# Two transformer blocks on one core: a norm's scale applied before the transposes, the second pair of memory heads inside an output chunk, and the last feed-forward's first chunk computed token tile by token tile

## The chip, the cores and the metric

The kernel runs on one core of one Trainium2 chip. The metric is device time in microseconds (us) of one launch. The kernel before took 786.58 us, the median of 3 runs (784.45, 786.58 and 787.6).

## The reference

256 tokens of width 1024 in fp32 go through two blocks. Block 1 mixes three branches (a gated linear recurrence, an mLSTM, a stick-breaking attention), then has a gated feed-forward of hidden width 2816 and a final norm. Block 2 mixes three other branches, then reads a memory of 256 rows through four heads of width 256, and then has a feed-forward of hidden width 4096 with a squared ReLU:

```python
def second_block(x, mem, ...):
    h = rms_norm(x, pre_mix_g)
    z = h @ w_in                                  # za, zb, zc
    ...
    x = x + rms_norm(y @ w_out, post_mix_g)
    h = rms_norm(x, pre_x_g)
    m = rms_norm(mem, mem_g)
    x = x + rms_norm(memory_cross_attention(h, m, w_xq, w_xkv, w_xo), post_x_g)
    h = rms_norm(x, pre_ffn_g)
    f = square(relu(h @ w_ff1)) @ w_ff2
    return x + rms_norm(f, post_ffn_g)

def memory_cross_attention(h, m, w_q, w_kv, w_o):
    q = (h @ w_q) in 4 heads; k, v = split(m @ w_kv) in 4 heads
    p = softmax(q k^T / 16)
    return (p v) @ w_o
```

`rms_norm(x, g)` is x divided by the root of its mean square over the width, times g.

## The kernel before, in words

**Tiles.** The 256 tokens are two tiles of 128 (t = 0, 1) in `x`. A product needs its input turned, with the model width on the partitions: 8 slices `kt` of 128 channels by 256 tokens, kept in `act_hl` as a rounded part ("high", fp32r) and a remainder ("low"). Quarter q of it holds slices 2q and 2q+1.

**Weights.** `plan_weights` cuts all weight matrices into groups of up to 1 MB, in the order in which they are used. Each group goes through four steps: SyncE loads it into one of 3 `raw` buffers; ScalarE copies it into one of 3 `high` buffers (`split_high`, line 702); VectorE, or GpSimd for some groups of the middle stretch, subtracts to get `low` (`split_low`, line 1217); TensorE uses it (`products`, line 1819) and counts up `w_used`. Each product is three matmuls (low by high, high by low, high by high). A `high` buffer is free when the group three before it is used, and a `raw` buffer when the group three before it has its `low`.

**Chunks.** A chunk is a column block of 512 outputs, in two groups of 4 slices each. `products` has modes: "T" puts tokens on the output's partitions and streams 512 weight columns (48 matmuls per chunk), "C" puts channels there and streams 256 tokens (96 matmuls), "S" is "C" with high and low inputs streamed as one operand, "F" is the second product of a feed-forward, which adds up in banks 4 to 7. `fresh=True` makes TensorE wait for `act_hl` quarter by quarter, `at=(kt, f)` runs f before slice kt's products, and `tile0=True` finishes token tile 0 of the last group ahead of tile 1, so that others can begin on it.

**Order.** All queues are written out by hand, one program per engine. ScalarE and VectorE call `ahead_of(key, mode)` (lines 1060 and 1660), which makes the high or low part of the group two places after each group of the chunk that TensorE is on; `ahead_of_half` does it for one half, and `hold=True` leaves out the last one, which is made later. An engine runs its queue strictly in order, so a group's split stands in front of whatever is written behind it.

**Norm 2** (the input of block 2's mix). After block 1's final norm (`final_norm`, line 1299), ScalarE squares x (`norm_stat(2)`), GpSimd makes `rstd`, and VectorE multiplies the identity by it (`norm_diag(2)`, line 1737) once per token tile. TensorE's `norm` (line 1948), which runs inside the product `("kv", 0)` ahead of slice 7 (line 2227), multiplies x by that diagonal matrix, so that turning and scaling are one matmul per slice and tile. `norm_split(2)` on ScalarE (line 773) and VectorE (line 1277) then makes high and low of `act_hl` from banks 4 to 7. On ScalarE four small transfers are issued at the end of `norm_stat(2)`; on VectorE both halves of `ahead_of(("kv", 0), "C")` come before `norm_split(2)`. The products of `zc` follow.

**Memory heads.** `x_scores(i)`, `x_turn(i)` and `x_out(i)` on TensorE (lines 2138 to 2168) work on heads 2i and 2i+1; between them ScalarE and VectorE do the softmax and the copies. Head h gives quarter h of `act_hl`. `x_scores(0)` runs inside `("xq", 1)`; the rest runs between that chunk and `("xo", 0)`, one after the other, lines 2269 to 2273.

**Feed-forward of block 2.** After the chunks `("xo", 0)` and `("xo", 1)`, ScalarE sums squares per tile (`post_in`), GpSimd makes a root, and VectorE computes the new x (`post_last(1)`, line 1634: `gain`, then `add_normed` in two halves, tile after tile). TensorE does 8 matmuls on the identity (`keep_warm(WARM[3])`, line 2276), turns x in halves as they come (`turn_halves(12)`), and runs the chunks `("up2", c)`, c = 0 to 7, and `("down2", c)`, each one behind. Chunks 0 and 1 of "up2" are in mode "C"; `hidden2(c)` makes ReLU, square, high and low from the two banks.

```python
            x_turn(0)
            x_scores(1)
            x_out(0)
            x_turn(1)
            x_out(1)
            for c in range(2):
                products(("xo", c), "T", fresh=c == 0, tile0=c == 1)
            keep_warm(WARM[3])
            turn_halves(12)
```

## Time and profile before

| what | us |
|---|---|
| median of 3 runs | 786.58 |
| lowest, highest | 784.45, 787.6 |
| the profiled execution, its own time | 784.17 |
| its span, first to last instruction | 782.4 |
| TensorE busy in it | 762.0 (97%) |
| TensorE's granted clock, mean | 0.999 of full |

The span is what the trace shows; the profiled execution's own time has 1.8 us more around it. "Busy" is time in which at least one instruction of the engine was under way. A row of the timeline gives the start, the length, the engine, the line, the operation, output and inputs, how many are merged (x32), and in brackets how long the engine had been idle before it and whom it waited for. Ends of matmuls are modelled: a row's length reaches a little past the start of the next one, so the pace of a run of matmuls is read from start to start. An fp32 matmul shows as two instructions, a transpose as one. Lines are often those of helpers (700 is every ScalarE activation, 1811 every matmul, 1909 every transpose, 1227 every low part), so that a row is told by its tiles.

### The profile page before, as it was taken

How to read it: one execution, taken by the hardware profiler on the slowest of the kernel's cores; microseconds unless marked ns; L12 is line 12 of the kernel's file. 1: busy time of each engine (PE TensorE's matmuls, PEld its weight loads, DVE VectorE, ACT ScalarE, POOL GpSimd, SP SyncE). 2: the span in 40 equal slices, each digit the busy share in tenths (PEclk: the TensorE clock that was granted, in tenths of full speed). 3: DMA queues.
4: the chain of work that ended last, by engine and by line, in shares of the span. 5: the costliest groups of instructions: out<-in, count | busy, mean ns of one | idle time of the engine just before them, and what ended most of it. 6: DMA issues, size and time to landing. Idle time of an engine off the chain costs nothing.

```text
span 782.4 us, 10603 instructions
## 1 busy us (share of the span) xinstructions
PE 762.0 (97%) x4411; PEld 665.8 (85%) x4411; DVE 512.9 (66%) x571; ACT 395.9 (51%) x493; POOL 77.9 (10%) x87
## 2 busy tenths in 40 slices
PE   8999999989999999999999999999999999999996
PEld 8978887868988888888899888789888988888885
DVE  5757964586666666666758989775546555666653
ACT  6375376534544445454554386664446434444441
POOL 3000003020000000000233422020003000000001
PEclk9999999999999999999999999999999999999999
DMA  9554554436465654566465435365234564645431
GB/s 308 186 207 146 176 200 168 155 108 214 154 201 179 208 175 162 165 213 215 164 213 163 162 130 188 117 221 185 103 108 139 212 213 166 211 170 187 164 127 54
DMA packets 74032, 135.67 MB, mean 173 GB/s; under 512 B 4458, under 2 KB 28928, under 8 KB 73984
## 3 DMA queue, kind: packets, MB, share of 16 engines
q1 hardware_dynamic: 72176, 130.80, 49.7%
q10 hardware_dynamic: 1808, 4.19, 1.7%
q8 instruction: 35, 0.57, 0.3%
q14 instruction: 13, 0.11, 0.0%
HBM read 133.93 MB, written 1.05 MB: 173 GB/s over the span
## 4 chain that ended last, share of the span: by engine, by line
PE 85%; DVE 6%; ACT 4%; issue 2%; DMA 2%; POOL 1%; ACTq 0%; DVEq 0%; POOLq 0%
PE wide L1811 60%; PE bank L1811 23%; DVE low L1227 2%; DMA raw<-in_w_in_dram 2%; ACT arena L700 2%; ACT high L700 1%; PE bank L1909 1%; POOL arena L623 1%; DVE act_hl L1283 1%; ACT xn L700 0%; DVE arena L1314 0%; DVE arena L1297 0%; DVE arena L1435 0%; DVE low L1267 0%; ACT act_hl L700 0%
## 5 line engine op out<-in xcount | busy, mean ns | idle before, releaser
L1227 DVE TENSOR_TENSOR low<-raw,high 128x2048 fp32r<-128x2048 f32 (+1 forms) x116 | 261.8, 2280 | 119.0 <-ACT high L700 118.2
L1811 PE MATMUL wide<-act_hl,high 128*128 128x256 f32 (+1 forms) x1248 | 308.7, 328 | 0.0
L700 ACT ACTIVATE high<-raw 128x2048 fp32r<-128x2048 f32 (+1 forms) x130 | 233.9, 1821 | 133.6 <-PE wide L1811 107.8
L1811 PE MATMUL wide<-act_hl,low 128*128 128x256 f32 x864 | 244.7, 283 | 3.1 <-DVE act_hl L1283 2.5
L1811 PEld LDWEIGHTS wide<-act_hl,high 128*128 128x128 f32 x1248 | 210.0, 190 | 22.3
L1811 PEld LDWEIGHTS wide<-act_hl,low 128*128 128x128 f32 x864 | 164.5, 190 | 4.4 <-DVE low L1227 1.6
L1811 PE MATMUL wide<-high,act_hl 128*128 128x512 f32 (+1 forms) x528 | 163.6, 387 | 2.9 <-DVE arena L1435 1.6
L1811 PEld LDWEIGHTS wide<-high,act_hl 128*128 128x128 f32 x528 | 98.2, 188 | 24.3 <-issue 3.7
L1811 PE MATMUL wide<-low,act_hl 128*128 128x512 f32 (+1 forms) x264 | 101.2, 383 | 0.0
L1811 PE MATMUL bank<-high,hid_l 128*128 128x512 f32 x216 | 84.8, 392 | 0.2 <-DVE hid_l L1502 0.2
L1811 PE MATMUL bank<-high,hid_h 128*128 128x512 f32 x216 | 84.4, 391 | 0.0
L1811 PE MATMUL bank<-low,hid_h 128*128 128x512 f32 x216 | 84.2, 390 | 0.0
L700 ACT ACTIVATE arena<-wide 128x512 f32<-128x512 f32 x59 | 32.7, 596 | 90.4 <-PE wide L1811 90.4
L1811 PEld LDWEIGHTS wide<-low,act_hl 128*128 128x128 f32 x264 | 49.6, 188 | 9.1
L553 POOL TENSOR_SCALAR var<-sums 128x1 f32<-128x1 f32 x10 | 7.1, 710 | 482.6 <-ACT arena L700 267.9
L1811 PEld LDWEIGHTS bank<-high,hid_l 128*128 128x128 f32 x216 | 40.6, 188 | 9.2 <-DVE hid_l L1502 0.6
L1811 PEld LDWEIGHTS bank<-high,hid_h 128*128 128x128 f32 x216 | 40.6, 188 | 8.9
L1811 PEld LDWEIGHTS bank<-low,hid_h 128*128 128x128 f32 x216 | 40.6, 188 | 8.0
L1811 PE MATMUL bank<-arena 128*128 128x256 f32 (+8 forms) x256 | 39.2, 341 | 3.2 <-POOL arena L623 1.1
L1314 DVE SCALAR_TENSOR_TENSOR arena<-arena,dw 128x256 f32<-128x256 f32 x60 | 40.2, 712 | 0.9
L1811 PEld LDWEIGHTS bank<-arena 128*128 128x128 f32 (+3 forms) x256 | 32.5, 179 | 9.1 <-POOL arena L623 1.6
L1483 DVE TENSOR_TENSOR arena<-wide,arena 128x512 f32<-128x512 f32 x30 | 20.7, 689 | 29.8 <-ACT arena L700 29.6
(195 smaller groups left out, 662.5 us busy)
## 6 DMA issues: line engine op xcount, KB each, us to landing
raw<-in_w_ff_dram SPq DMA_DIRECT2D x32, 1024.0 KB, 5.3
raw<-in_w_in_dram SPq DMA_DIRECT2D x28, 1024.0 KB, 5.4
raw<-in_w_ffn_in_dram SPq DMA_DIRECT2D x44, 512.0 KB, 4.9
raw<-in_w_ffn_out_dram SPq DMA_DIRECT2D x11, 1024.0 KB, 6.7
raw<-in_w_xkv_dram SPq DMA_DIRECT2D x8, 1024.0 KB, 5.1
raw<-in_w_o_dram SPq DMA_DIRECT2D x4, 1024.0 KB, 5.1
raw<-in_w_out_dram SPq DMA_DIRECT2D x4, 1024.0 KB, 5.2
raw<-in_w_xq_dram SPq DMA_DIRECT2D x4, 1024.0 KB, 4.9
```

What stands on the lines that cost most here:

```text
L553: pool.tensor_scalar(v, sums[:, t, 0:1], sums[:, t, 1:2], EPS, ALU.add, ALU.add)\
L623: pool.affine_select(out=part_a, in_=part_a, compare_op=ALU.is_gt, fill=0.0, base=0, pattern=[[0, 4], [1, P]], channel_multiplier=-1).then ...
L700: return act.activation(dst, src, func, **k)
L1227: tt(part(low, g), part(raw, g), f32(part(high, g)), SUB).then_inc(sem.low_by_dve, 1)
L1283: ins = stt(l_, bank[4 + q][:, k * T:(k + 1) * T], col(NORM_GAIN[n], kt), f32(h_), MUL, SUB)
L1314: ins = stt(tile_of(dst, c), window, weight(j, c), tile_of(dst, c), MUL, ADD)
L1483: tt(in2(h_low[b]), wide_of(b, 0), in2(h_low[b]), ADD).then_inc(sem.hid_sum, 1)
L1811: return pe.matmul(dst, lhs, rhs, start=start, stop=stop, skip_group_check=loose)
L1909: return pe.transpose(dst, src, ident[0:n, 0:n])
```

## The change

Three places change.

1. **Norm 2.** VectorE's `norm_diag(2)` gives way to `scale_x()`, which writes x times `rstd` into `xn`, one instruction of 128x1024 per token tile. TensorE turns `xn` with 16 transposes (`turn_scaled`) at the same point, ahead of slice 7 of `("kv", 0)`. ScalarE makes the high part of zc's first group ahead of `norm_stat(2)`, and issues its four small transfers (`load_block2`) behind the high part of the second. VectorE makes only the first low part ahead of `norm_split(2)` and the second behind it.
2. **Heads.** `x_turn(1)` and `x_out(1)` move into `("xo", 0)`, ahead of slices 2 and 4. `x_scores` waits for its own head's queries alone. VectorE and ScalarE put the splits of the next groups between the halves.
3. **Feed-forward.** `keep_warm(WARM[3])` goes. `("up2", 0)` is computed with tokens on the partitions, first all of tile 0 and then all of tile 1 (`up_by_token`); the turns of tile 1's halves stand inside it. Its result is squared by token (`hidden_tok`), turned by 8 transposes inside `("up2", 1)` (`turn_hidden`), and split from there (`hidden_turned`). ScalarE and VectorE split `act_hl` by token tile (`split_tile`), VectorE's first two quarters of tile 0 ahead of `add_normed` of tile 1. The splits of both groups of `("up2", 0)` now come before `post_last(1)`, as `hold` is gone.

```diff
-WARM = 4, 4, 6, 8
+WARM = 4, 4, 6
@@ scalar
+            def split_tile(t):
+                if t == 0:
+                    act.wait_ge(sem.w_used, me.used)
+                tok = slice(t * P, (t + 1) * P)
+                for q in range(4):
+                    act.wait_ge(sem.turned, me.seen("turned"))
+                    for k in range(2):
+                        kt = 2 * q + k
+                        ins = f(split_of(kt, False)[0][:, tok], bank[4 + q][:, k * T + t * P:k * T + (t + 1) * P], ACT.Copy,
+                                scale=col(NORM_GAIN[5], kt))
+                    ins.then_inc(sem.act_h, 1)
...
             norm_stat(FINAL)
+            ahead_of_half(("kv", 0), 0)
             norm_stat(2)
-            ahead_of_half(("kv", 0), 0)
             ahead_of_half(("kv", 0), 1)
+            load_block2()
             norm_split(2)
...
             x_out(0)
+            ahead_of_half(("xo", 0), 0)
             x_turned(1)
             x_out(1)
-            for c in range(2):
-                ahead_of(("xo", c), "T", hold=c == 1)
-                post_in(c)
-            split_high(me.used + LEAD)
-            norm_split(5)
+            ahead_of_half(("xo", 0), 1)
+            post_in(0)
+            ahead_of(("xo", 1), "T")
+            post_in(1)
+            split_tile(0)
+            split_high(me.used + LEAD + 1)
+            split_tile(1)
             norm_stat(5)
+            ahead_of(("up2", 0), "T")
+            hidden_tok()
+            ahead_of_half(("up2", 1), 0)
+            hidden_turned()
+            ahead_of_half(("up2", 1), 1)
+            hidden2(1)
+            ahead_of(("down2", 0), "F")
@@ vector
+            def scale_x():
+                for t in range(TT):
+                    dve.wait_ge(sem.rstd, me.seen("rstd"))
+                    ts(xn[:, t, :], x[:, t, :], rstd[:, 4 + t:5 + t], None, MUL).then_inc(sem.scaled, 1)
...
-            norm_diag(2)
-            ahead_of(("kv", 0), "C")
+            scale_x()
+            ahead_of_half(("kv", 0), 0)
             norm_split(2)
+            ahead_of_half(("kv", 0), 1)
...
-            x_out()
-            ahead_of(("xo", 0), "T")
+            x_out(0)
+            ahead_of_half(("xo", 0), 0)
+            x_out(1)
+            ahead_of_half(("xo", 0), 1)
             post_first()
-            ahead_of(("xo", 1), "T", hold=True)
-            post_last(1)
-            norm_split(5, (0, 1))
-            split_low(me.used + LEAD)
-            norm_split(5, (2, 3))
+            ahead_of(("xo", 1), "T")
+            post_last(1, lambda: split_tile(0, (0, 1)))
+            split_tile(0, (2, 3))
+            split_low(me.used + LEAD + 1)
+            split_tile(1, range(4))
             dve.wait_ge(sem.rstd, me.seen("rstd", TT))
+            ahead_of(("up2", 0), "T")
+            hidden_tok()
+            ahead_of_half(("up2", 1), 0)
+            hidden_turned()
+            ahead_of_half(("up2", 1), 1)
+            hidden2(1)
+            ahead_of(("down2", 0), "F")
@@ tensor
+            def turn_scaled():
+                for t in range(TT):
+                    pe.wait_ge(sem.scaled, 0 + t + 1)
+                    turn_x(t, range(KD), t == 1, xn)
+
+            def up_by_token():
+                pair = 2 * (me.pairs % 2)
+                parts = chunks[("up2", 0)]
+                for t in range(TT):
+                    tok = slice(t * P, (t + 1) * P)
+                    for g, kts in parts:
+                        if t == 0 and kts[0]:
+                            turn_half(1, 0)
+                        pe.wait_ge(low_sem(g), before(g))
...
+                            if kt % 2 == 0:
+                                pe.wait_ge(sem.act_hl, me.seen("act_hl"))
...
+                        if t:
+                            ins.then_inc(sem.w_used, 1)
+                        elif kts[0]:
+                            ins.then_inc(sem.tok_used, 1)
+                            turn_half(1, 1)
...
-                    pe.wait_ge(sem.xq_in, 2 + 2 * (h // 2))
+                    pe.wait_ge(sem.xq_in, h + 1)
...
-            products(("kv", 0), "C", is_mem=True, at=(KD - 1, norm))
+            products(("kv", 0), "C", is_mem=True, at={KD - 1: turn_scaled})
...
             x_out(0)
-            x_turn(1)
-            x_out(1)
+            products(("xo", 0), "T", fresh=True, at={2: lambda: x_turn(1), 4: lambda: x_out(1)})
+            products(("xo", 1), "T", tile0=True)
             for c in range(2):
-                products(("xo", c), "T", fresh=c == 0, tile0=c == 1)
-            keep_warm(WARM[3])
-            turn_halves(12)
+                turn_half(0, c)
+            up_by_token()
+            products(("up2", 1), "C", at={4: turn_hidden})
+            pe.wait_ge(sem.hid_hl, n1 + 2)
+            products(("down2", 0), "F", 0, last=False)
             n2 = F2 // NB
-            for c in range(n2 + 1):
+            for c in range(2, n2 + 1):
```

## Rows read from the trace of the kernel before

**Rows 1.** The page's first part: busy us, share of the span, instructions of each engine.
```profile
PE 762.0 (97%) x4411; PEld 665.8 (85%) x4411; DVE 512.9 (66%) x571; ACT 395.9 (51%) x493; POOL 77.9 (10%) x87
```

**Rows 2.** Timeline of TensorE at norm 2, 392 to 400 us.
```profile
393.23 3.74 PE L1811 MATMUL bank<-diag,x 128*128 128x128 f32 x32
396.73 0.36 PE L1811 MATMUL wide<-hid_h,low 128*128 128x256 f32 x1
...
398.12 0.28 PE L1811 MATMUL wide<-hid_h,high 128*128 128x256 f32 x1
399.83 0.36 PE L1811 MATMUL wide<-act_hl,low 128*128 128x256 f32 x1 [1.44 <-DVE act_hl L1283]
```

**Rows 3.** Timeline of TensorE, 16 transposes inside another product, 520 to 524 us.
```profile
522.04 1.91 PE L1909 MATMUL bank<-ident,x 128*128 128x128 f32 x16
523.70 0.48 PE L1811 MATMUL wide<-high,hid_l 128*128 128x512 f32 x1
```

**Rows 4.** Timelines of VectorE, ScalarE and GpSimd at norm 2, 386 to 402 us.
```profile
393.97 4.94 DVE L1227 TENSOR_TENSOR low<-raw,high 128x2048 fp32r<-128x2048 f32 x2 [1.69 <-ACT high L700]
398.82 3.21 DVE L1283 SCALAR_TENSOR_TENSOR act_hl<-bank,vec,act_hl 128x256 fp32r<-128x256 f32 x8
...
392.02 3.71 ACT L700 ACTIVATE high<-raw 128x2048 fp32r<-128x2048 f32 x2 [1.03 <-issue]
395.73 3.03 ACT L700 ACTIVATE act_hl<-bank,vec 128x256 fp32r<-128x256 f32 x8
...
391.38 0.57 POOL L564 TENSOR_TENSOR rstd<-var,neg_half 128x1 f32<-128x1 f32 x1
```

**Rows 5.** Groups by line and shape, VectorE: a TENSOR_SCALAR from SBUF to SBUF.
```profile
L1386 DVE TENSOR_SCALAR arena<-arena 128x512 f32<-128x512 f32 x1 | 0.4, 421 | 0.0
```

**Rows 6.** Timeline of TensorE at the memory heads, 556 to 571 us.
```profile
557.73 7.17 PE L1811 MATMUL bank<-arena 128*128 128x256 f32 x32 [0.54 <-DVE arena L1297]
564.74 1.04 PE L1909 MATMUL bank<-ident,arena 128*128 128x128 f32 x8
566.57 3.72 PE L1811 MATMUL bank<-arena 128*128 128x256 f32 x16 [0.79 <-ACT arena L700]
569.93 0.58 PE L1811 MATMUL wide<-high,act_hl 128*128 128x512 f32 x1
```

**Rows 7.** Timeline of VectorE at the heads: the low part of quarter 0.
```profile
564.00 0.68 DVE L1447 SCALAR_TENSOR_TENSOR act_hl<-bank,act_hl 128x512 fp32r<-128x512 f32 x1
```

**Rows 8.** Timeline of TensorE between the chunks xo and up2, 588 to 600 us.
```profile
591.94 1.95 PE L1811 MATMUL bank<-ident 128*128 128x128 f32 x16
593.72 2.38 PE L1909 MATMUL bank<-ident,x 128*128 128x128 f32 x16
597.21 0.35 PE L1811 MATMUL wide<-act_hl,low 128*128 128x256 f32 x1 [1.11 <-DVE act_hl L1283]
```

**Rows 9.** Timelines of VectorE, ScalarE and GpSimd in the same stretch.
```profile
591.26 1.41 DVE L1628 SCALAR_TENSOR_TENSOR x<-xn,rstd,x 128x512 f32<-128x512 f32 x2 [0.44 <-POOL rstd L564]
...
597.76 2.28 DVE L1227 TENSOR_TENSOR low<-raw,high 128x2048 fp32r<-128x2048 f32 x1
...
590.20 0.30 POOL L553 TENSOR_SCALAR var<-sums 128x1 f32<-128x1 f32 x1 [59.90 <-ACT arena L700]
...
599.47 0.66 POOL L556 TENSOR_SCALAR var<-sums 128x1 f32<-128x1 f32 x1 [5.60 <-ACT xn L700]
```

**Rows 10.** The chain that ended last: chunks xo 0 and 1 ("T"), up2 0 and 1 ("C").
```profile
570.29 21.81 PE wide L1811 x96
...
597.21 23.27 PE wide L1811 x192
```

**Rows 11.** Timeline of TensorE, 170 to 173 us: a stretch of transposes and waiting.
```profile
170.39 1.09 PE L1909 MATMUL bank<-ident,xn 128*128 128x128 f32 x8
172.61 0.47 PE L1811 MATMUL wide<-high,act_hl 128*128 128x512 f32 x1 [1.13 <-DVE act_hl L1447]
```

**Rows 12.** Busy us of each engine in 166 to 173 us; PEclk is the granted clock.
```profile
166.00:173.00 7.00, 5.87 (x30) 4.63 (x30) 4.94 (x9) 1.86 (x3) 3.18 (x3) 1.00 0.35 129
```

More of the change, by code:

```diff
@@ L147, in __init__ @@
         self.hid_t = new("hid_t")
+        self.hid_turned = new("hid_turned")
         self.ident = new("ident")
@@ L202, in __init__ @@
         self.rstd = new("rstd")
+        self.scaled = new("scaled")
         self.sb_a = new("sb_a")
@@ L213, in __init__ @@
         self.sumsq = new("sumsq")
+        self.tok_used = new("tok_used")
         self.turned = new("turned")
@@ L785, in norm_split, with hidden_tok, hidden_turned @@
                     ins.then_inc(sem.act_h, 1)
+            def split_tile(t):
[9 more added lines that the diff above has]
+                    ins.then_inc(sem.act_h, 1)
+            def hidden_tok():
+                for t, b in enumerate(me.pair()):
+                    if t:
+                        act.wait_ge(sem.w_used, me.used)
+                    else:
+                        act.wait_ge(sem.tok_used, 1)
+                    f((h_act, h_tmp)[t], b[:, :], ACT.Relu).then_inc(sem.hid_t, 1)
+            def hidden_turned():
+                act.wait_ge(sem.hid_a, me.seen("hid_a", 2))
+                for b in range(2):
+                    act.wait_ge(sem.hid_turned, b + 1)
+                    f(flat(hid_h[0][:, 2 * b:2 * b + 2, :]), bank[4 + b][:, :], ACT.Copy).then_inc(sem.hid_h, 1)
             def first_stat(t):
@@ L1288, in norm, with split_tile @@
                 norm_split(n)
+            def scale_x():
+                for t in range(TT):
+                    dve.wait_ge(sem.rstd, me.seen("rstd"))
+                    ts(xn[:, t, :], x[:, t, :], rstd[:, 4 + t:5 + t], None, MUL).then_inc(sem.scaled, 1)
+            def split_tile(t, quarters):
+                tok = slice(t * P, (t + 1) * P)
+                for q in quarters:
+                    dve.wait_ge(sem.act_h, me.seen("act_h"))
+                    for k in range(2):
+                        kt = 2 * q + k
+                        h_, l_ = (half[:, tok] for half in split_of(kt, False))
+                        ins = stt(l_, bank[4 + q][:, k * T + t * P:k * T + (t + 1) * P], col(NORM_GAIN[5], kt), f32(h_), MUL, SUB)
+                    ins.then_inc(sem.act_hl, 1)
             def rep_wait():
@@ L1452, in turn_merged, with x_out @@
                     low_of_bank(q, 0.5)
-            def x_out():
-                for q in range(4):
+            def x_out(i):
+                for q in (2 * i, 2 * i + 1):
                     low_of_bank(q)
@@ L1524, in hidden2, with hidden_tok, hidden_turned @@
                     dve.wait_ge(sem.hid_hl, me.seen("hid_hl"))
+            def hidden_tok():
+                for t in range(TT):
+                    h = (h_act, h_tmp)[t]
+                    dve.wait_ge(sem.hid_t, me.seen("hid_t"))
+                    tt(h, h, h, MUL).then_inc(sem.hid_a, 1)
+            def hidden_turned():
+                for b in range(2):
+                    dve.wait_ge(sem.hid_h, me.seen("hid_h"))
+                    tt(flat(hid_l[0][:, 2 * b:2 * b + 2, :]), bank[4 + b][:, :], f32(flat(hid_h[0][:, 2 * b:2 * b + 2, :])), SUB)\
+                        .then_inc(sem.hid_hl, 1)
+                dve.wait_ge(sem.hid_hl, me.seen("hid_hl", 2))
             def za_in():
@@ L1632, in post_first, with post_last @@
                     gain(b, t, 0)
-            def post_last(i):
+            def post_last(i, then=None):
                 for t, b in enumerate(me.pair()):
                     gain(b, t, 1)
+                    if t and then:
+                        then()
                     add_normed(i, t)
@@ L1956, in norm, with turn_x @@
                             ins.then_inc(sem.turned, 1)
-            def turn_x(t, kts, last):
+            def turn_x(t, kts, last, src=x):
                 for kt in kts:
                     o = (kt % 2) * T + t * P
-                    ins = turn(bank[4 + kt // 2][:, o:o + P], x[:, t, kt * P:(kt + 1) * P])
+                    ins = turn(bank[4 + kt // 2][:, o:o + P], src[:, t, kt * P:(kt + 1) * P])
                     if last and kt % 2:
@@ L2169, in _ @@
             turn_start()
-            products("lru", "C", fresh=True, at=(6, rep_made))
+            products("lru", "C", fresh=True, at={6: rep_made})
             vectors()
@@ L2264, in _ @@
             pe.wait_ge(sem.zg, 2)
-            products(("kv", 3), "T", is_mem=True, at=(4, lambda: turn_all(10)))
-            products(("xq", 0), "C", fresh=True, at=(4, rep_made))
+            products(("kv", 3), "T", is_mem=True, at={4: lambda: turn_all(10)})
+            products(("xq", 0), "C", fresh=True, at={4: rep_made})
             pe.wait_ge(sem.kv_in, 8)
-            products(("xq", 1), "C", at=(4, lambda: x_scores(0)))
+            products(("xq", 1), "C", at={4: lambda: x_scores(0)})
             x_turn(0)
```

49 lines of the change are left out of this document (33 added, 16 removed).

## The prediction

> **What bounds the kernel now.** I read the page's first part first: TensorE is busy 762.0 of 782.4 us, VectorE 66% and ScalarE 51% [rows 1]. So time is to be had from only two sources: work that TensorE does and need not do, and its few waits. I then went through TensorE's timeline for the rows with a bracket (a wait) and read the three places of the change, with the other engines' timelines beside it to see what each wait hangs on.
>
> Norm 2: 32 instructions on the diagonal, 393.23 to 396.73, the last products of ("kv", 0), then a wait on VectorE until 399.83 [rows 2]. VectorE spends 4.94 us on two low parts and only then, at 398.82, splits the quarter for which TensorE waits, though ScalarE has offered it since some 396.5 (start 395.73, two of eight instructions in 3.03) [rows 4]. Heads: a wait of 0.54 for scaled queries and one of 0.79 for ScalarE's copies [rows 6]. Feed-forward: from 591.94 to 597.21 TensorE does matmuls on the identity, 16 transposes that come as x comes, and waits 1.11 [rows 8].
>
> **Part 1, norm 2.** *TensorE's work.* 32 diagonal instructions from start to the next start: 3.50 us [rows 2]. 16 transposes of the same size inside another product: 522.04 to 523.70, 1.66 us [rows 3]. Saved: 1.84.
>
> *Is the scaled x there in time?* GpSimd has the second root at 391.38 + 0.57 = 391.95 [rows 4]. No row shows a TENSOR_SCALAR of 128x1024. A 128x512 one takes 0.42 [rows 5], so twice that, 0.84, is the upper bound if the pace holds, and 0.42 the lower one; I take 0.7. It ends at 392.7, and TensorE asks at 393.23. Covered by the products of slices 0 to 6; the cover is 0.5 us wide. (ScalarE's high part, moved ahead of the squares, takes 3.71/2 = 1.86 us [rows 4] and delays the first root; the second tile's square waits for VectorE's final norm anyway, so I leave the second root where it is.)
>
> *The wait.* The first quarter is turned after 10 of 16 transposes, 393.23 + 1.04 = 394.3. ScalarE ended its squares at 392.02 - 1.03 = 391.0 [rows 4]. Now it makes zc's second high part (to 392.9) and issues the four transfers, which before fitted under a square and that 1.03 of idle; if they run one behind the other they end at 394.7. Its first quarter is then ready at about 395.3 (2 x 0.38). VectorE makes one low part from 392.7, 2.3 us, to 395.0, splits at once (2 x 0.40) and is done at 396.2. TensorE ends ("kv", 0) at 393.23 + 1.66 + (398.24 - 396.73) = 396.4. The wait of 399.83 - 398.24 = 1.59 (the bracket's 1.44 plus modelled ends) goes.
>
> *What is late next.* zc's second low part now comes behind the split, from 398.7 to 401.0; TensorE needs it half a chunk after 396.4, at 402.2. 1.2 us to spare. GpSimd's masks come some 3 us later and nothing waits on them for 30 us. Gain 1.84 + 1.59 = 3.4; I take 3.3, with ends 2.8 (scaling at 1.3 a tile, the transfers in the open) and 3.4.
>
> **Part 2, heads.** With h + 1 in the wait, x_scores(1) starts one scaling instruction sooner: 0.54 gone. x_turn(1) and x_out(1) cost TensorE what they cost now, but the wait of 0.79 for two copies [rows 6] lies under slices 2 and 3 (12 matmuls, 21.81/96 = 0.227 each, 2.7 us [rows 10]). New is that slice 0 needs quarter 0 at once: its low part ends at 564.68 [rows 7], and TensorE is free of x_out(0) at 564.74 [rows 6]; both move alike, so 0 to 0.1 is lost. Quarter 2 is asked for right after x_out(1): its head is done 1.8 us earlier (half of 3.36, 566.57 to 569.93), copy and low part take 0.6 and 0.69, so it is there 0.4 us before. Gain 1.33 less 0.1: 1.2, ends 0.9 and 1.33.
>
> **Part 3, feed-forward.** All in the old frame, with the chunk xo ending at 591.94. Without `hold`, up2's second low part (2.28 us [rows 9]) runs on VectorE as soon as the first half of ("xo", 1) is used, 591.94 - 5.45 = 586.5: high to 588.4, low to 590.7. Behind it in VectorE's queue stands `gain` for tile 0, whose sum was there at 590.20 [rows 9]: 0.55 us late. GpSimd's root waits with it. The row shows why: the same small operation takes 0.30 at 590.20 and 0.66 at 599.47, where it ends as VectorE's low part ends [rows 9]. So tile 0's halves of x come at 592.4 and 593.1 instead of 591.96 and 592.67.
>
> By the Trainium skill (GPSIMD Engine Reference, Specifications) GpSimd shares its SBUF interfaces with VectorE, with contention where VectorE has two SBUF inputs; that speaks against this part of the change. The 0.66 row agrees. Without the rule the root would come 0.4 sooner and the sum would gain 0.4.
>
> TensorE turns the halves up to 593.6 (8 transposes, 0.10 each). ScalarE's first two 128-token copies end about 593.5 (0.25 to 0.38 each), VectorE's gain of tile 1 at 593.75, its two half-size split instructions (0.2 to 0.4 each, half of 0.40 and all of it) at about 594.3. up2 starts at 594.4 instead of 597.21: 2.8 earlier.
>
> Then TensorE's own bill. The eight transposes of tile 1 move inside the chunk, +0.83; the eight of `turn_hidden` are new, +0.83; the chunk in "T" instead of "C" saves (23.27 - 21.81)/2 = 0.73 [rows 10]. Net +0.93. Tile 1 must be in time: VectorE's queue behind 594.3 is a quarter (0.5), add_normed (1.41), two quarters (1.1), a low part (2.3), four quarters (2.2), 7.5 us in all, to 602.4 at the latest pieces; TensorE reaches tile 1's last quarters at 603.5. 1.1 us to spare. `hidden_tok` and the splits of ("up2", 1) end before TensorE gets to slice 4 of that chunk at about 612. Gain 2.8 - 0.9 = 1.9; I take 1.8. Low end 0.6 (the slack used up once), high end 2.2.
>
> Sum: 3.3 + 1.2 + 1.8 = 6.3 us. The profiled execution took 784.17, so 777.9 in its terms. It lies 2.4 below the median of the runs, 786.58; from there the same gain gives 780.3. A measurement of this kernel can tell about 0.5%, 3.9 us, from no change; the threshold is 782.65.
>
> **Rivals.**
> *A, the clock falls (slower).* The plain matmuls on the identity go, and from 591.94 to 594.4 TensorE only waits or transposes, 2.46 us. If the granted clock then fell from 2.4 to 1.2 GHz for the chunk that follows, its 10.9 us would double and the sum turn to 6.3 - 10.9 = -4.6: 791.2. It decides for "slower" from 6.3 us of work at the lower clock on. Against it: from 170.39 to 172.61 there are 8 transposes and a wait and no other matmul, 2.2 us, and the clock stays at 1.00 [rows 11, 12]. The new stretch is 0.24 longer than that, and would be longer still if VectorE is late.
> The Trainium skill speaks for it (TensorE: Matmul & The Clock Gate, PE-mode transpose): transposes do not count as busy for the clock as matmuls do. By that rule the whole of both stretches is idle; the 1.00 in the row shows that 2.2 us of it are borne. I give it 0.06.
>
> *B, part 1 is eaten.* The middle stretch leans on VectorE, which also shares ports with GpSimd's low parts there; if zc's second low part comes later than 402.2, or the later collisions fall worse, the 3.3 shrink to nothing and 3.0 remain: 783.6. Against: VectorE's work there hangs on the end of zc's products and should move with it. 0.12.
>
> *C, part 3 gives nothing.* The queue order (low part before gain, split before add_normed) makes TensorE wait inside the chunk for tile 1: 4.5 remain, 782.1. 0.14.
>
> *D, the change does not do what it says,* transposes of xn costing what the diagonal did (-1.84) and waits merely moving: total 2 or less, 784.6 or more. Rows 3 speak against. 0.06.
>
> **How the numbers follow.** Forecast 0.62. Small ends of the parts: 2.8 + 0.9 + 0.6 = 4.3, 782.3; large ends 3.4 + 1.33 + 2.2 = 6.9, 779.7. The runs scatter by 2.1 below and 1.0 above their median, so a median of a few by about 1.5. The range reaches from 778.2 to 784.2: it takes in B and C and leaves out A and most of D. Faster by over 0.5%: forecast, most of C, a third of B, 0.74. Within: the rest of B, C, D, 0.20. Slower: A, 0.06.
>
> **What would show it.** Right: 16 transposes and no bank<-diag instruction at norm 2, and less than 0.2 us before zc's first matmul; no bracket over 0.2 at the heads, x_out(1) inside ("xo", 0); up2's first matmul 2.3 to 2.7 us behind xo's last; clock 1.00 there. Wrong: a bracket on tile 1's quarters or on a low part inside zc or up2; new waits of TensorE between 450 and 500 us; a total that moves by under 4 us with all three places as described.

## The result, and the profile after

| | before | after |
|---|---|---|
| median, us (runs) | 784.45 (5) | 778.45 (5) |
| lowest, highest | 784.15, 787.6 | 777.98, 780.04 |
| profiled execution | 784.17 | 777.98 |
| its span | 782.4 | 776.2 |

The ratio is 0.9919, 95% interval 0.9902 to 0.9936: faster by 0.8%. In a second set of runs the changed kernel gave 778.06 (777.95 to 780.06, 5 runs) beside 784.62, ratio 0.9919 [0.9907, 0.9932]; one execution of the kernel before in that set took 2681.08 us and is left out of the ratio. Profiled execution against profiled execution the gain is 784.17 - 777.98 = 6.2 us; the forecast was 6.3. The time forecast, 780.3, is 1.85 too high all the same: it was counted down from 786.58, and the kernel before does not stand there (its two further runs gave 784.4 and 784.15).

The page's first part of the changed kernel; against [rows 1] TensorE has 72 instructions and 3.4 us of work less:

```profile
PE 758.6 (98%) x4339; PEld 660.3 (85%) x4339; DVE 514.0 (66%) x579; ACT 396.9 (51%) x501; POOL 74.3 (10%) x87
```

**Norm 2.** Timelines of TensorE, then VectorE, of the changed kernel, to be held against [rows 2 to 5]:

```profile
393.08 1.91 PE L1995 MATMUL bank<-ident,xn 128*128 128x128 f32 x16
394.75 0.36 PE L1897 MATMUL wide<-hid_h,low 128*128 128x256 f32 x1
...
396.33 0.36 PE L1897 MATMUL wide<-act_hl,low 128*128 128x256 f32 x1
```

```profile
391.95 0.76 DVE L1337 TENSOR_SCALAR xn<-x,rstd 128x1024 f32<-128x1024 f32 x1 [0.76 <-POOL rstd L567]
392.62 2.29 DVE L1271 TENSOR_TENSOR low<-raw,high 128x2048 fp32r<-128x2048 f32 x1
395.31 3.23 DVE L1327 SCALAR_TENSOR_TENSOR act_hl<-bank,vec,act_hl 128x256 fp32r<-128x256 f32 x8 [0.40 <-ACT act_hl L703]
398.45 2.28 DVE L1271 TENSOR_TENSOR low<-raw,high 128x2048 fp32r<-128x2048 f32 x1
```

The 32 instructions of 3.50 us are 16 transposes of 1.67, and zc's first matmul has no bracket. VectorE splits at 395.31 where it split at 398.82, since one low part (392.62) and not two stand ahead of it; the other comes at 398.45.

**Heads.** TensorE, against [rows 6]: no bracket, and x_turn(1) stands between matmuls of the output chunk.

```profile
552.71 1.04 PE L1995 MATMUL bank<-ident,arena 128*128 128x128 f32 x8
553.69 7.17 PE L1897 MATMUL bank<-arena 128*128 128x256 f32 x32
560.79 0.47 PE L1897 MATMUL wide<-high,act_hl 128*128 128x512 f32 x1
...
563.63 1.03 PE L1995 MATMUL bank<-ident,arena 128*128 128x128 f32 x8
564.42 0.48 PE L1897 MATMUL wide<-high,act_hl 128*128 128x512 f32 x1
```

**Feed-forward.** TensorE, VectorE and GpSimd, against [rows 8, 9]:

```profile
586.83 0.39 PE L1897 MATMUL wide<-high,act_hl 128*128 128x512 f32 x1
587.85 1.32 PE L1995 MATMUL bank<-ident,x 128*128 128x128 f32 x8 [0.63 <-DVE x L1702]
589.80 0.47 PE L1897 MATMUL wide<-high,act_hl 128*128 128x512 f32 x1 [0.63 <-DVE act_hl L1346]
...
592.61 0.60 PE L1995 MATMUL bank<-ident,x 128*128 128x128 f32 x4
592.97 0.48 PE L1897 MATMUL wide<-high,act_hl 128*128 128x512 f32 x1
```

```profile
583.82 2.29 DVE L1271 TENSOR_TENSOR low<-raw,high 128x2048 fp32r<-128x2048 f32 x1 [2.05 <-ACT high L703]
586.03 0.69 DVE L1694 TENSOR_TENSOR xn<-wide,row_g 128x512 f32<-128x512 f32 x1
587.04 1.42 DVE L1702 SCALAR_TENSOR_TENSOR x<-xn,rstd,x 128x512 f32<-128x512 f32 x2 [0.32 <-POOL rstd L567]
```

```profile
585.32 0.96 POOL L556 TENSOR_SCALAR var<-sums 128x1 f32<-128x1 f32 x1 [58.47 <-ACT arena L703]
```

The warming matmuls are gone, two waits of 0.63 stand in their place, and the chunk up2 begins 2.97 us behind xo's last matmul (before: 5.50). The turns of tile 1 stand inside it, without a wait. GpSimd's small operation begins as ScalarE has its sum and takes 0.96: it ends at 586.28, shortly behind VectorE's low part (583.82 + 2.29 = 586.11). In the kernel before, where no low part runs beside it, it takes 0.30 [rows 9].

**Where the time went.** Each stretch from start to start in the timelines of TensorE: from the first matmul of ("kv", 0) to zc's first, from x_turn(0) to xo's last matmul, from there to up2's first, from there to down2's first.

| stretch | before | after | difference | forecast |
|---|---|---|---|---|
| norm 2 | 16.67 | 13.32 | -3.35 | -3.3 |
| zc to x_turn(0) | 156.32 | 156.38 | +0.06 | 0 |
| heads and xo | 35.56 | 34.12 | -1.44 | -1.2 |
| xo to up2 | 5.50 | 2.97 | -2.53 | -2.8 |
| up2 to down2 | 23.10 | 24.31 | +1.21 | +0.93 |

These add up to 6.05 us. The other 0.15 of the 6.2 lies ahead of norm 2, where nothing was changed: ("kv", 0) begins at 383.01 and not 383.16. Behind down2's first matmul both kernels take 154.96 to the last one.

### The profile page after: what moved, and what is told of

Read it like the earlier page. It is cut to its first block, busy times and chain, and to the rows that moved or that the text cites. A ratio compares the mean times of both kernels' runs of the same rounds, so it can differ in the third digit from the quotient of the medians.

```text
span 776.2 us, 10478 instructions
## 1 busy us (share of the span) xinstructions
PE 758.6 (98%) x4339; PEld 660.3 (85%) x4339; DVE 514.0 (66%) x579; ACT 396.9 (51%) x501; POOL 74.3 (10%) x87
## 3 DMA queue, kind: packets, MB, share of 16 engines
HBM read 133.93 MB, written 1.05 MB: 174 GB/s over the span
## 4 chain that ended last, share of the span: by engine, by line
PE 88%; DVE 5%; ACT 2%; DMA 1%; POOL 1%; issue 1%; DVEq 0%; ACTq 0%; POOLq 0%
PE wide L1897 63%; PE bank L1897 24%; PE bank L1995 2%; DMA raw<-in_w_in_dram 1%; ACT arena L703 1%; DVE low L1271 1%; ACT high L703 1%; POOL arena L626 1%; DVE x L1702 0%; DVE act_hl L1327 0%; DVE arena L1373 0%; DVE arena L1494 0%; DVE low L1311 0%; DVE xn L1694 0%; DVE arena L1624 0%
## 5 line engine op out<-in xcount | busy, mean ns | idle before, releaser
L1897 PE MATMUL wide<-act_hl,high 128*128 128x256 f32 (+1 forms) x1184 | 297.2, 330 | 0.0
L1897 PE MATMUL wide<-act_hl,low 128*128 128x256 f32 x832 | 235.8, 283 | 0.5 <-DVE low L1311 0.5
L1897 PEld LDWEIGHTS wide<-act_hl,high 128*128 128x128 f32 x1184 | 200.1, 190 | 22.3
L1897 PE MATMUL wide<-high,act_hl 128*128 128x512 f32 (+1 forms) x560 | 174.7, 388 | 3.4 <-DVE arena L1494 1.6
L1897 PEld LDWEIGHTS wide<-act_hl,low 128*128 128x128 f32 x832 | 158.5, 190 | 1.6 <-DVE low L1311 0.7
L1897 PEld LDWEIGHTS wide<-high,act_hl 128*128 128x128 f32 x560 | 104.2, 188 | 26.4 <-issue 4.5
L1897 PE MATMUL wide<-low,act_hl 128*128 128x512 f32 (+1 forms) x280 | 107.5, 384 | 0.0
L1897 PEld LDWEIGHTS wide<-low,act_hl 128*128 128x128 f32 x280 | 52.7, 188 | 9.6
```

Of the source, the lines that this page charges most:

```text
L1897: return pe.matmul(dst, lhs, rhs, start=start, stop=stop, skip_group_check=loose)
```

## The experiments

### Each part alone

Both edits of norm 2 were tried one at a time on the kernel before.

```diff
@@ n2_turn: the transposes, without the new order
-            norm_diag(2)
+            scale_x()
...
-            products(("kv", 0), "C", is_mem=True, at=(KD - 1, norm))
+            products(("kv", 0), "C", is_mem=True, at=(KD - 1, turn_scaled))
@@ n2_order: the order, with the diagonal
-            norm_stat(2)
             ahead_of_half(("kv", 0), 0)
+            norm_stat(2)
             ahead_of_half(("kv", 0), 1)
+            load_block2()
...
-            ahead_of(("kv", 0), "C")
+            ahead_of_half(("kv", 0), 0)
             norm_split(2)
+            ahead_of_half(("kv", 0), 1)
```

> The kernel before with the scaled x turned plainly, and all orders of ScalarE and VectorE as before. Theory S (VectorE's queue set the wait): TensorE saves 1.84 us of work ahead of the last products of (kv, 0) but still waits for VectorE, which makes both low parts first; zc starts at 399.8 as before, the bracket grows from 1.44 to about 3.2, and the whole time is unchanged to 0.2 us. Rival W (the work itself was the cost): zc starts 1.8 us sooner, at 398.0.

> The kernel before with only the new order of ScalarE and VectorE at norm 2 (one low part ahead of the split, one behind it, the high part ahead of the squares, the four transfers later); the diagonal matmuls stay. Theory S: the wait of 1.44 (1.6 from start to start) goes, zc starts at 398.3, 1.5 to 1.6 us sooner, and the total falls by as much. Together with the other half that makes 3.4, where the halves alone give 0 and 1.6. Rival W: the order gives nothing by itself, the diagonal's 3.5 us being what made VectorE late; zc at 399.8.

`n2_turn` took 786.84 us (783.96 to 789.16, 10 runs), ratio 1.0018 [1.0002, 1.0034]. TensorE got its 1.8 us back and spent them on the same wait, behind which its clock fell. Timeline of TensorE, then busy time in windows of 2 us (the last three columns are the granted clock, the DMA share and GB/s):

```profile
395.01 0.36 PE L1817 MATMUL wide<-hid_h,low 128*128 128x256 f32 x1
...
399.96 0.56 PE L1817 MATMUL wide<-act_hl,low 128*128 128x256 f32 x1 [3.28 <-DVE act_hl L1284]
```

```profile
398.00:400.00 2.00, 0.04 (x1) 0.07 (x1) 2.00 (x4) 2.00 (x6) 1.43 (x2) 0.82 0.88 317
400.00:402.00 2.00, 2.00 (x9) 2.00 (x10) 2.00 (x6) 1.54 (x1) 0.00 (x0) 0.50 1.02 380
```

zc's first matmul came 16.69 us behind ("kv", 0)'s (before: 16.67), and the clock went from 2.4 to 1.2 GHz until 406 us, so that x_turn(0) stood 159.0 behind it and not 156.3. With the wait of 1.44 [rows 2] the kernel before has 1.00 in all these windows. `n2_order` took 783.48 (782.68 to 784.66, 6 runs), ratio 0.998 [0.9967, 0.9994]: the stretch is 15.08, 1.59 less, with no bracket. Alone the transposes give nothing and the order 1.59; together they give 3.35. That is part 1's sum of 1.84 and 1.59, but only in this pair.

```diff
@@ heads_only: on the kernel before
+            ahead_of_half(("xo", 0), 0)
             x_turned(1)
             x_out(1)
...
-                    pe.wait_ge(sem.xq_in, 2 + 2 * (h // 2))
+                    pe.wait_ge(sem.xq_in, h + 1)
...
-            x_turn(1)
-            x_out(1)
...
+            products(("xo", 0), "T", fresh=True, at=(2, lambda: x_turn(1), 4, lambda: x_out(1)))
@@ ff_only: on the kernel before, all of part 3
-            keep_warm(WARM[3])
-            turn_halves(12)
...
+            up_by_token()
+            products(("up2", 1), "C", at={4: turn_hidden})
```

> The kernel before with only the heads' part of the change. Theory S: two waits go, the span falls by 1.2 to 1.4 us, and the chunk xo ends 1.2 to 1.4 us sooner after the start of xq. Rival: the fp32 matmuls of the head put between fp32r products slow both, and less than 0.8 is left.

> The kernel before with only the feed-forward's part of the change. Theory S as corrected by the trace after: up2 starts 2.5 to 2.7 us sooner after xo's last matmul (2.7 instead of 5.3), 1.2 us of that are spent again up to the start of (down2, 0), and the span falls by 1.3 to 1.5 us. Rival (the parts lean on each other): alone it gives less than 0.8, since the heads' part is what makes VectorE free in time.

`heads_only` took 784.34 (782.32 to 784.99, 10 runs), 0.9985 [0.9974, 0.9995]; `ff_only` 784.15 (782.76 to 785.13, 10 runs), 0.9988 [0.9977, 0.9998]. Their traces have the stretches of the changed kernel: 34.12 for heads and xo in the one, 2.97 and 24.35 for xo to up2 and up2 to down2 in the other. So the two parts don't lean on each other: -1.44, and 27.32 - 28.60 = -1.28. The medians alone (0.40 and 0.59 under 784.74) would have made the parts look like a third and a half of that: six and five of the ten executions have a mean clock of 0.995 or 0.996, and these lie 1 to 2 us above the others.

### The clock between xo and up2

```diff
@@ no_warm: on the kernel before
-            keep_warm(WARM[3])
@@ warm_back: on the changed kernel, ahead of tile 0's turns
             products(("xo", 1), "T", tile0=True)
+            keep_warm(8)
```

> The kernel before without the eight matmuls on the identity behind xo. From xo's last product to up2's first, 5.2 us, TensorE then only turns x and waits. Rival A of the prediction (the clock falls): the granted clock drops to 1.2 GHz behind that stretch, matmuls of 512 columns step by more than 0.4 us instead of 0.23 for a while, and the kernel is slower than before by 1 us or more. Theory S: the clock stays at 1.00, the transposes wait for x as before, and the time changes by less than 0.2 us.

> The changed kernel with the eight matmuls on the identity put back behind xo. Theory S: they take 1.8 us, x's first half is ready after 0.8 of them, so up2 starts 0.9 to 1.1 us later than in the changed kernel and the span grows by that, at the same clock. Rival A: they keep the clock up, and the span is equal or shorter.

`no_warm` took 786.38 (784.53 to 788.05, 10 runs), 1.0014 [1.0, 1.0028]. Timeline of TensorE, then its windows:

```profile
592.61 1.32 PE L1909 MATMUL bank<-ident,x 128*128 128x128 f32 x8
595.32 1.32 PE L1909 MATMUL bank<-ident,x 128*128 128x128 f32 x8 [1.39 <-DVE x L1628]
597.75 0.55 PE L1811 MATMUL wide<-act_hl,low 128*128 128x256 f32 x1 [1.11 <-DVE act_hl L1283]
```

```profile
596.00:598.00 2.00, 0.89 (x5) 0.68 (x6) 1.27 (x4) 2.00 (x6) 0.00 (x0) 0.79 0.10 39
598.00:600.00 2.00, 2.00 (x10) 2.00 (x11) 2.00 (x2) 2.00 (x6) 0.00 (x0) 0.50 0.67 223
600.00:602.00 2.00, 2.00 (x17) 2.00 (x16) 2.00 (x5) 2.00 (x3) 1.73 (x4) 0.86 0.24 33
```

Rival A's mechanism is real: behind 5.1 us of transposes and waits the clock goes to 0.50, and up2 to down2 grows from 23.10 to 24.35. By the Trainium skill (TensorE: Matmul & The Clock Gate, Part 4, PE-mode transpose) transposes do not count as busy for the clock the way matmuls do. The trace agrees with that and does not prove it: the two waits alone, 1.39 and 1.11, are shorter than the one of 2.11 us at 41.98 us, behind which the clock of the same trace stays at 1.00. What the forecast had too large is the price, 1.25 us and not 10.9: the clock is back at 0.86 in the window from 600 us and at 1.00 in the next. In the changed kernel the same stretch is 2.97 long and the clock stays:

```profile
588.00:590.00 2.00, 1.36 (x9) 0.92 (x9) 2.00 (x6) 1.61 (x7) 1.14 (x2) 1.00 0.96 393
590.00:592.00 2.00, 2.00 (x10) 1.64 (x10) 2.00 (x6) 2.00 (x4) 0.00 (x0) 1.00 0.18 72
```

`warm_back` took 779.63 (779.11 to 780.78, 4 runs), 0.9929 [0.9911, 0.9947]: up2's first matmul stands 3.91 behind xo's last, 0.94 later, and the clock is 1.00 as it was without. By token tiles the warmers are all cost.

### What sets up2's first matmul

```diff
@@ quarters_first: on the changed kernel
-            post_in(1)
-            split_tile(0)
+            post_in(1, lambda: split_tile(0, (0, 1)))
+            split_tile(0, (2, 3))
...
-                    gain(b, t, 1)
                     if t and then:
                         then()
+                    gain(b, t, 1)
@@ low_late: on the changed kernel
-            ahead_of(("xo", 1), "T")
+            ahead_of(("xo", 1), "T", hold=True)
             post_last(1, lambda: split_tile(0, (0, 1)))
+            split_low(me.used + LEAD)
```

> The changed kernel with ScalarE's copies of tile 0's quarters 0 and 1 ahead of its squares of tile 1, and VectorE's split of them ahead of tile 1's gain. Theory Q (the queue order of ScalarE and VectorE sets the start of up2): up2 starts at 588.8 instead of 589.8, 1.0 us sooner; tile 1's x then comes 1.1 us later, at 591.2 to 591.9, TensorE waits up to 0.5 for it inside the chunk, and 0.4 to 0.8 us of the span remain. Rival: the wait only moves inside the chunk and the span is the same to 0.2 us.

> The changed kernel with VectorE's low part of up2's second group put behind add_normed of tile 1 instead of ahead of tile 0's gain. Theory Q: gain of tile 0 starts at 585.3 instead of 586.03, GpSimd's first operation takes 0.3 instead of 0.96 us, and x's first half is ready 0.7 us sooner; but the low part ends at 593 to 594.5 and pushes quarters 2 and 3 behind it, so that TensorE waits 1.5 to 2.5 us at slice 4: slower by 1 to 2 us in all. Rival: the low part fits into VectorE's idle time there and the span falls by 0.5.

`quarters_first` took 779.22 (778.65 to 780.57, 4 runs), 0.9924 [0.9906, 0.9942]: up2's first matmul stands 2.98 behind xo's last, as in the changed kernel, so neither tile 1's gain nor ScalarE's order is what it waits for, and behind it 0.39 is lost. `low_late` took 780.26 (779.21 to 781.8, 4 runs), 0.9934 [0.9909, 0.9959]. Its rows of GpSimd, then TensorE's rows with a bracket:

```profile
587.33 0.30 POOL L556 TENSOR_SCALAR var<-sums 128x1 f32<-128x1 f32 x1 [58.49 <-ACT arena L703]
```

```profile
591.33 0.47 PE L1898 MATMUL wide<-high,act_hl 128*128 128x512 f32 x1 [0.82 <-DVE act_hl L1346]
...
595.89 0.47 PE L1898 MATMUL wide<-high,act_hl 128*128 128x512 f32 x1 [1.11 <-DVE act_hl L1346]
```

With VectorE's low part out of the way GpSimd's operation takes 0.30 in place of 0.96 and up2 begins 2.50 behind xo, 0.47 sooner. Two things come sooner here, the root and tile 0's gain (by 0.77, as it stood behind the same low part); the bracket of 0.32 on the root in the changed kernel says that GpSimd was the later of the two there. The low part then stands ahead of tile 0's later quarters: TensorE waits 1.11 inside the chunk, up2 to down2 takes 25.72 and not 24.31, and the kernel ends 0.94 later than the changed one. The 0.96 agrees with the rule on shared SBUF interfaces that the forecast named (the Trainium skill, GPSIMD Engine Reference, Specifications); the forecast's own row for it was 0.66. The 0.30 at 587.33 has a VectorE instruction beside it too, the gain at 587.26, but one that reads a bank and only one input from SBUF.

### Two levels of time

In all sets of runs so far some executions lie 1.5 to 2 us above the rest, about two in three of them at a mean clock of 0.996 or less, where those of the rest are 0.997 to 0.999. A mean of 0.997 by itself says nothing: the trace of `both` below has it without a fall, because the clock is at 0.50 in the last 4 us, where TensorE has no work left, and that of `before_warm_41` has it with one. Two places that the change does not touch showed a fall. One is behind a wait in the first 42 us. Timeline and windows of `quarters_first`, where nothing of this had been edited:

```profile
41.95 0.60 PE L1997 MATMUL bank<-ident,arena 128*4 128x128 f32 x4 [2.05 <-ACT arena L703]
```

```profile
42.00:44.00 2.00, 2.00 (x9) 1.60 (x10) 1.95 (x3) 0.01 (x1) 0.00 (x0) 0.67 0.78 297
44.00:46.00 2.00, 2.00 (x7) 1.52 (x6) 0.00 (x0) 1.95 (x3) 0.00 (x0) 0.50 0.86 238
```

The same wait is 2.11 us in `no_warm`, and there the clock stays at 1.00: it falls in some executions and not in others. The first remedy was matmuls on the identity in that wait, alone on both kernels, and in `best` together with an edit of the section before, VectorE's low part cut in halves around tile 0's quarters.

```diff
@@ warm_41 (on the changed kernel), before_warm_41 (on the kernel before)
             products("ifsv", "T", width=264)
+            keep_warm(7)
             if_rows()
@@ best: the changed kernel, keep_warm(7) as above, and
-            ahead_of(("xo", 1), "T")
+            ahead_of(("xo", 1), "T", hold=True)
...
-            post_last(1, lambda: split_tile(0, (0, 1)))
-            split_tile(0, (2, 3))
+            low_half(0)
+            post_last(1, lambda: split_tile(0, (0, 1)), lambda: (split_tile(0, (2, 3)), low_half(1)))
+            split_tile(1, (0, 1))
             split_low(me.used + LEAD + 1)
-            split_tile(1, range(4))
+            split_tile(1, (2, 3))
```

> The changed kernel again, for more executions with their granted clocks. Theory K (two levels): each execution is either at a mean clock of 0.997 to 0.999 and about 778.3 us, or at 0.995 to 0.996 and about 779.9, and the second level comes from a fall of the clock behind TensorE's wait at 41 us, which stands in the kernel before as well. Rival F: the change has made a second place for it, behind xo, and then a third level of about 781.5 at 0.993 appears, or a profile shows half clock at 590 to 600 us.

> The changed kernel with seven matmuls on the identity at 39.7 us, inside TensorE's wait of 1.8 us for ScalarE ahead of the turns of if_tok. They take 1.56 us and should delay nothing. Theory K: the lower level vanishes, every execution is at 0.997 or more and at 778.0 to 778.7 us; the fastest are not faster than the changed kernel's. Rival F: the levels stay as they are, since the fall sits elsewhere.

> The kernel before with the same seven matmuls at 39.7 us. Theory K: its executions gather at 784.0 to 784.5 us, and those of 785.5 to 787.6, about two in five, vanish; the median falls by up to 0.5 us, the mean by 0.7. Rival F: no difference.

> The changed kernel with the seven matmuls at 39.7 us, and with VectorE's low part of up2's second group in two halves: one ahead of tile 0's gain, one behind tile 0's split, which now stands between the two halves of add_normed of tile 1; the split of tile 1's first quarters goes ahead of the next low part. Theory Q as mended by quarters_first and low_late (what sets up2's start is the first half of x, which waits for GpSimd's root, which waits for VectorE's low part): up2 starts 2.5 us behind xo's last matmul instead of 2.97, and 0.3 to 0.5 us of the span go against warm_41. Rival: the half low part still holds GpSimd up, or the queue behind it gives the gain back inside the chunk; the same span to 0.1 us.

`after_again` is the second set given above: seven of the ten executions of the changed kernel lie at 777.95 to 778.45, three at 779.67 to 780.06. `warm_41` gave 779.59 (778.01 to 780.52, 6 runs), three executions on each level; `before_warm_41` 785.75 (784.05 to 786.54, 11 runs), 1.0006 [0.9996, 1.0016]; `best` 779.47 (777.93 to 779.94, 5 runs), 0.9926 [0.9913, 0.9939]. The levels stayed, with three of six, six of eleven and three of five executions among the upper times, so the wait is not the only place. (As to `best`'s other edit, its up2 begins 2.50 behind xo and the part from there to down2 takes 24.42, so that 0.36 is gained in the trace.) The trace of `best` shows the other place. Timeline of TensorE, then windows:

```profile
66.77 0.41 PE L2010 MATMUL bank<-ident,arena 4*128 4x4 f32 x4
67.04 1.97 PE L1912 MATMUL bank<-arena 4*128 4x256 f32 x8
68.94 0.50 PE L1912 MATMUL wide<-high,act_hl 128*128 128x512 f32 x1
```

```profile
68.00:70.00 2.00, 2.00 (x9) 1.47 (x8) 1.96 (x8) 0.91 (x1) 0.00 (x0) 0.93 1.05 388
70.00:72.00 2.00, 2.00 (x6) 1.52 (x6) 1.96 (x6) 1.99 (x7) 0.00 (x0) 0.50 0.52 200
```

TensorE is busy all through and waits for nothing; but for 2.2 us its matmuls and transposes use 4 of the 128 partitions, and then the clock is at 0.50. Four other profiled executions (n2_order, heads_only, low_late, before_warm_41) fell here too. From the 4x4 transposes to ("kv", 0)'s first matmul it is 318.56 to 318.62 us in these five, and 316.96 to 317.01 in the profiles of before, after and seven others: a fall costs 1.6 us there. In the kernel before 0.4 of it comes back at norm 2, whose stretch is 16.23 and 16.26 and not 16.67 in heads_only and before_warm_41; without that wait, in the changed kernel, nothing comes back (13.31 and 13.32 in best and low_late). So the stretch was split: heads 2 and 3 ahead of slice 2 of the next chunk.

```diff
@@ split_67 (on the changed kernel); both adds keep_warm(7); before_both is both edits on the kernel before, best_both on best
-                for h in range(4):
+                mlstm_rows((0, 1))
+
+            def mlstm_rows(heads):
+                for h in heads:
...
-            products(("gate", 0), "T")
+            products(("gate", 0), "T", at={2: lambda: mlstm_rows((2, 3))})
```

> The changed kernel with the small matmuls of heads 2 and 3 (contraction over 4 partitions, four of the eight at 66.8 to 68.9 us) issued ahead of slice 2 of the gate instead of beside those of heads 0 and 1. Theory (the clock falls in one of two places, behind the wait that ends at 41.95 us or behind this stretch): the falls at 68 to 74 us are gone and those at 42 to 48 us stay, so both levels stay, with fewer executions at the lower one; the upper level is 778.0 to 778.5 us, the lower 779.6 to 780.6. Rival (the stretch has nothing to do with the falls): a profile or its like still shows the clock at 0.50 at 68 to 74 us, and the share of the lower level is as in the changed kernel (2 in 10 so far). Moving the matmuls costs 0.2 us at most.

> The changed kernel with seven warmers in the wait that ends at 41.95 us and with the small matmuls split as in split_67. Theory: both places are mended, so every execution has a mean granted clock of 0.997 or more and lies at 778.0 to 778.7 us; the median is 778.2. Rival (the falls come from elsewhere, or from the chip and not from the kernel): executions at 0.993 to 0.996 remain, 779.6 to 780.6 us, some in five or more.

> The kernel before with the same two edits as in both. Theory: every execution lies at 784.0 to 784.6 us with a mean clock of 0.997 or more, and the executions of the kernel before at 785.5 to 787.6 are missing. Rival: the share of the upper times is as in the kernel before (about a third to a half).

> The variant with two half low parts ahead of the chunk and the warmers at 41 us, with the small matmuls split too. Theory: every execution at 777.6 to 778.0 us, so 0.3 to 0.4 us under both, as its trace already gave between the last matmul of the output chunk and the first of the down projection (26.92 against 27.28 us). Rival: executions at 779.4 to 780 us remain.

| kernel | median | lowest, highest | runs | ratio |
|---|---|---|---|---|
| split_67 | 778.72 | 778.37, 779.09 | 4 | 0.992 [0.9906, 0.9934] |
| both | 778.59 | 778.28, 778.94 | 5 | 0.9917 [0.9904, 0.9931] |
| best_both | 778.29 | 778.01, 778.56 | 4 | 0.9914 [0.9901, 0.9928] |
| before_both | 784.65 | 784.12, 785.92 | 11 | 0.9998 [0.9989, 1.0007] |
| before, beside them | 784.83 | 783.4, 786.21 | 15 | |

None of the 13 executions of the three variants of the changed kernel is among the upper times or under a clock of 0.997. Of the 21 of after, after_again, warm_41 and best nine were at 779.47 or more, six of these under 0.997. The sets ran on different chips, but the kernel before, run beside the 13, still had four of 15 at 0.995 or 0.996. The warmers at 41 us, which stand in nine of the 13, can't be what did it: warm_41 and best have them too. Windows of `both`, where `best` fell:

```profile
68.00:70.00 2.00, 2.00 (x9) 1.66 (x10) 1.97 (x8) 0.00 (x0) 0.00 (x0) 1.00 1.05 399
70.00:72.00 2.00, 2.00 (x9) 1.18 (x9) 1.97 (x6) 0.00 (x0) 0.00 (x0) 1.00 0.39 151
```

Expected was that split_67 alone would keep the falls at 42 us; none came in its four runs, which settles little about that place. Whether it is the 4 partitions or the length of the stretch that matters was not tried. The edit costs more than the 0.2 us allowed: 317.40 in place of 316.96 to 317.01 in all four, 0.43, since each return to the products costs some 0.1 and each group of four takes 1.05 us where eight took 1.90. So it takes away the scatter and does not lower the median: best_both, the fastest of the three, is not told apart from the changed kernel (778.45 and 778.06).

before_both came out half as expected: its clock is 0.997 or more in all 11, but they reach to 785.92. Its profiled execution, 785.49, shows another source of scatter. It comes to the 4x4 transposes at 67.08 and not 66.20, and 784.17 + 0.88 + 0.44 = 785.49. The 0.88 comes early: the first product's matmul starts at 10.03 in place of 9.40, and at 34.58 stands a wait of 0.37 for a low part that before has not. Timelines of the kernel before, then of `both`, where that first matmul starts at 10.50:

```profile
5.62 1.91 PE L1909 MATMUL bank<-ident,x 128*128 128x128 f32 x16
7.37 1.50 PE L1811 MATMUL wide<-ident 128*128 128x128 f32 x12
```

```profile
5.64 3.21 PE L1995 MATMUL bank<-ident,x 128*128 128x128 f32 x16
8.69 1.50 PE L1897 MATMUL wide<-ident 128*128 128x128 f32 x12
10.50 0.39 PE L1897 MATMUL wide<-act_hl,low 128*128 128x256 f32 x1 [0.31 <-DVE low L1311]
```

It is no late transfer: x lands 3.8 and 4.6 us after its two issues in the kernel before and 3.7 and 4.5 in `both`, the first weights 5.6 and 5.3. The same 16 transposes of x take 1.75 us in the one and 3.05 in the other, 0.11 and 0.19 each, and what follows moves with them: in all 18 traces the first product starts 1.8 to 2.03 us behind their end, and so between 9.17 (quarters_first) and 10.51 us (before_warm_41). The slower pace is about that of half the clock, and the matmuls on the identity ahead of these transposes step by 0.23 in both (3.78 to 5.62 and 5.64) where those at 591.94 step by 0.11 [rows 8]. The windows read 1.00 for both, but the trace's record of the clock only begins, at 1.00, at 5.6 us in the kernel before and at 8.3 in `both`, so they can't tell. That TensorE starts at the lower level and leaves it sooner or later is therefore likely and was not tried by an edit.

## Why the prediction was right and where it was wrong

- **Part 1, right.** 3.35 against 3.3: 16 transposes 1.67 (1.66 taken), the scaling 0.75 a tile (0.7 taken), zc's second low part from 398.45 (398.7). ScalarE issued the four transfers beside its square and its high part (390.07 to 391.9), and its first quarter waited for TensorE's transposes (from 394.43), not for them.
- **Part 2, right, a little low.** 1.44 against 1.2. Start to start the two waits were worth 0.60 and 1.04, more than their brackets, less 0.1 for each of two returns to the products; the loss set down for slice 0 did not come. (Half of 3.36 is 1.7 and not 1.8; the 0.4 us to spare that it led to is right.)
- **Part 3, mis-sized.** 1.32 against 1.8. "2.8 earlier" was 2.53: GpSimd's operation took 0.96 and not 0.66 beside the low part. So the sign "2.3 to 2.7 us behind xo's last" was missed, with 2.97 from start to start. "Net +0.93" was +1.21: the two rows of the chain [rows 10] hold modelled ends, and from start to start the chunk in "T" saves 0.66 and not 0.73 (23.10 against 96 steps of 0.227, halved), and each of three returns from transposes to matmuls costs some 0.1, for which the sum had nothing. "1.1 us to spare" held: no bracket inside.
- **The step that failed** is "It lies 2.4 below the median of the runs, 786.58; from there the same gain gives 780.3". A median of three executions was taken as the kernel's level. Two of the three, 786.58 and 787.6, lie 2 and 3 us above the third, and the runs put the level lower: 784.45 over 5 executions, and 784.62 to 785.06 in four later sets of 13 to 27. The sum of 6.3 taken from 784.45 gives 778.15, where 778.45 was measured, so nearly all of the 1.85 us by which 780.3 is off is this step and not the mechanism. Traces of other executions show what can lift one by such an amount, a fall of the clock or a slow start; the three themselves have no trace, so for them this is argued.
- **Luck.** From the profiled execution, 777.9 was right to 0.1, and this is in part luck: the stretches add up to 6.05 and not 6.3, with part 2 better and part 3 worse than set down, and 0.15 came from scatter ahead of norm 2.
- **Rivals.** A: the mechanism is shown (no_warm, n2_turn), its price was four to nine times too high (10.9 us against 2.7 in n2_turn and 1.25 in no_warm), and the changed kernel stays clear of it. B falls: zc to x_turn(0) is 156.38, and the shift is rigid. C falls: no wait inside up2. D falls: 16 transposes cost 1.67 and not 3.50; its "waits merely moving" is true of the transposes alone (n2_turn), but not of the pair.

## What to carry to other kernels

Take work off an engine and off its wait together: the transposes alone gave a longer wait and then a lower clock, in the pair 3.35 us. A gain that was worked out in one trace holds from that execution's own time. Three runs with a gap of 2 us between them may stand on different levels, and then their median is no centre: take more runs before a forecast is counted down from it. Where a bound engine's instruction waits for a small GpSimd operation, look at what VectorE does beside it.

## What the runs showed of the hardware

TensorE's clock fell behind a stretch in which it was never idle: 2.2 us of matmuls and transposes on 4 partitions, then 1.2 GHz for some 3 us, 1.6 us lost, in some executions and not in others. By the Trainium skill (TensorE: Matmul & The Clock Gate, Part 1) the clock goes by how busy the engine has been; here the busy column was 2.00 of 2.00, so what the profile calls busy is not what the clock goes by. A 128x1 operation of GpSimd took 0.96 us beside a 128x2048 low part of VectorE and 0.30 beside a gain that reads a bank. And TensorE's first 16 transposes took from 1.74 to 3.05 us, without x landing later in the two traces held against each other, so that the first product started anywhere from 9.17 to 10.51 us.
